# Value copies taken bank by bank during their unit, an output weight rounded ahead of the exponentials, and another order of output fills

## The reference, cut to what matters

```python
def dilated_attention_mixer(x, positions, k_sh, v_sh, w_q, w_o):
    q = rope((x @ w_q).reshape(...), positions)
    for g, (window, dilation) in enumerate(BRANCHES):   # (128,1), (512,4), (2048,16)
        o, lse = dilated_branch(q[:, :, g], k_sh[:, :, g], v_sh[:, :, g], window, dilation)
        ...
    wts = jax.nn.softmax(jnp.stack(lses, axis=0), axis=0)
    o = jnp.einsum("gbsh,gbshd->bshd", wts, jnp.stack(outs, axis=0))
    return o.reshape(B, S, N_HEADS * HEAD_DIM) @ w_o
```

## Time and profile before

| | us |
|---|---|
| median of 3 runs | 2104.25 (2101.3 to 2106.06) |
| the profiled execution's own time | 2102.27 |
| its span | 2100.5 |
| TensorE busy | 2063.2 (98% of the span) |
| VectorE busy | 1162.4 (55%) |
| ScalarE busy | 707.0 (34%) |

### The profile page before, as it was taken

The page is one execution under the profiler, slowest core; times in us unless marked ns, Lnnn a source line. Parts: engine busy times, 40 slices in busy tenths (PEclk is TensorE's granted clock), DMA queues, the critical chain, the costliest instruction groups (busy, mean ns, idle before and its releaser), DMA issues.

```text
span 2100.5 us, 26015 instructions
## 1 busy us (share of the span) xinstructions
PE 2063.2 (98%) x10218; PEld 1722.3 (82%) x10218; DVE 1162.4 (55%) x1954; ACT 707.0 (34%) x1088; POOL 9.7 (0%) x23
## 2 busy tenths in 40 slices
PE   8999999999999999999999999999999899999998
PEld 6888888888888898898887888888888678888886
DVE  6646444422774766757757744442398866444323
ACT  4224322221522323333234422231344563222213
POOL 0000000000000000000000000000000000000000
PEclk9999999999999999999999999999999999999999
DMA  5862222222124142151332122222222122222221
GB/s 175 117 112 81 100 100 100 100 100 96 67 104 135 61 129 72 61 140 61 108 94 68 59 95 100 100 100 100 100 102 81 41 100 81 100 86 95 101 98 60
DMA packets 37193, 198.53 MB, mean 95 GB/s; under 512 B 3911, under 2 KB 7016, under 8 KB 15736
## 3 DMA queue, kind: packets, MB, share of 16 engines
q1 hardware_dynamic: 28192, 179.91, 24.6%
q10 hardware_dynamic: 7992, 14.80, 3.1%
q0 software_dynamic: 928, 2.70, 2.6%
HBM read 181.14 MB, written 3.67 MB: 88 GB/s over the span
## 4 chain that ended last, share of the span: by engine, by line
PE 92%; DVE 4%; ACT 2%; issue 1%; DMA 0%; ACTq 0%; DVEq 0%
PE bank L1670 79%; PE bank L1711 5%; PE bank L1989 2%; PE bank L1951 1%; PE bank L1967 1%; PE bank L1700 1%; ACT w_hi L544 1%; DVE work L1005 0%; DVE w_lo L957 0%; DVE w_lo L959 0%; PE bank L2225 0%; PE bank L2130 0%; PE bank L2006 0%; DVE work L1070 0%; DVE h L1073 0%
## 5 line engine op out<-in xcount | busy, mean ns | idle before, releaser
L1670 PE MATMUL bank<-x_hi,w_hi 128*128 128x512 f32 x1564 | 619.9, 396 | 0.0
L1670 PE MATMUL bank<-x_hi,w_lo 128*128 128x512 f32 x1564 | 609.8, 390 | 0.0
L1670 PE MATMUL bank<-x_lo,w_hi 128*128 128x512 f32 x1564 | 609.3, 390 | 0.0
L957 DVE TENSOR_TENSOR w_lo<-w_raw,w_hi 128x2048 fp32r<-128x2048 f32 (+1 forms) x143 | 300.8, 2111 | 427.6 <-ACT w_hi L544 427.4
L544 ACT ACTIVATE w_hi<-w_raw 128x2048 fp32r<-128x2048 f32 (+1 forms) x132 | 249.9, 1895 | 341.2 <-PE bank L1670 318.5
L1670 PEld LDWEIGHTS bank<-x_hi,w_hi 128*128 128x128 f32 x1564 | 294.0, 188 | 65.2 <-issue 5.9
L1670 PEld LDWEIGHTS bank<-x_hi,w_lo 128*128 128x128 f32 x1564 | 293.8, 188 | 62.7
L1670 PEld LDWEIGHTS bank<-x_lo,w_hi 128*128 128x128 f32 x1564 | 294.3, 188 | 60.0 <-issue 1.4
L1670 PE MATMUL bank<-ff_hi,w_hi 128*128 (+2 forms) x542 | 208.1, 384 | 0.0
L1670 PE MATMUL bank<-ff_lo,w_hi 128*128 (+2 forms) x542 | 207.9, 384 | 0.0
L1670 PE MATMUL bank<-ff_hi,w_lo 128*128 (+2 forms) x542 | 207.9, 384 | 0.0
(11 more groups left out here) (225 smaller groups left out, 2295.4 us busy)
## 6 DMA issues: line engine op xcount, KB each, us to landing
w_raw<-w_all SPq DMA_DIRECT2D x167, 1024.0 KB, 4.9
qk<-qk_next ACTq DMA_DIRECT2D x32, 384.0 KB, 10.7
w_raw<-w_all SPq DMA_DIRECT2D x6, 256.0 KB, 8.7
h<-x_t ACTq DMA_DIRECT2D x3, 512.0 KB, 7.3
skew<-erow POOLq DMA_DIRECT2D x8, 192.0 KB, 8.8
out_t<-h SPq DMA_DIRECT2D x3, 512.0 KB, 3.0
bias<-skew POOLq DMA_DIRECT2D x8, 128.0 KB, 6.3
w_raw<-w_all SPq DMA_DIRECT2D x4, 128.0 KB, 3.7
```

What stands on the lines that cost most here:

```text
L957: ins = v.tensor_tensor(w_lo[p][:, part], raw, hi, ALU.subtract)
L1670: ins = mm(out, b if flip else a, a if flip else b, start=start and n == 0, stop=stop and n == 2, **kw)
```

## The change

`v12_unit` signals a new semaphore `v12_bank` when half 1 has finished banks 4, 5 and 6. VectorE takes those three quarters in a new `take_v12_banks`, which stands ahead of the group's start and waits bank by bank; each take counts in `v12_taken`. Only quarter 3 is taken inside the attention, at entry S1. TensorE's single wait before MAXPERM becomes three: for quarter 0 before MAXPERM, for quarters 0 and 1 before the first transpose, and for all four before the first product with the values. In the last group ScalarE rounds `ATT_OUT + 1` right behind `ATT_OUT`, ahead of the exponentials; VectorE makes its rest after entry S0, not S1; and the first four fills go half 0 of rows 0, half 0 of rows 1, half 1 of rows 0, half 1 of rows 1.

```diff
--- before.py
+++ after.py
@@ -220,6 +220,8 @@
 
 def fill_of(n):
 
+    if FILL_A <= n < FILL_A + 4:
+        return 0, (n - FILL_A) % 2, (n - FILL_A) // 2
     if FILL_A <= n < FILL_A + 2 * KC:
         return 0, (n - FILL_A) // 2, (n - FILL_A) % 2
     if FILL_B <= n < FILL_B + KC:
@@ -405,6 +407,8 @@
         at_av = sem("at_av")
         at_rl = sem("at_rl")
         at_out = sem("at_out")
+        v12_bank = sem("v12_bank")
+        v12_taken = sem("v12_taken")
         b_row = sem("b_row")
         b_rowcopied = sem("b_rowcopied")
         b_scores = sem("b_scores")
@@ -757,12 +761,11 @@
             for b in range(6):
                 mix_hi_block(b)
             round_unit(ATT_OUT)
+            round_unit(ATT_OUT + 1)
             for n, (pair, names) in enumerate(GROUP_STEPS):
                 for name in names:
                     attend(3, pair, name)
-                if n == 0:
-                    round_unit(ATT_OUT + 1)
-                elif n == 19:
+                if n == 19:
                     mix_hi_block(6)
                 if n == 27:
                     act.wait_ge(at_scores, 8 * KC)
@@ -1293,8 +1296,13 @@
             def take_v12(t):
                 for br in (1, 2):
                     ins = take_v(br, t, V12_BANKS[t][:, (br - 1) * 256:br * 256])
-                if t == 3:
-                    ins.then_inc(evac, 1)
+                ins.then_inc(evac if t == 3 else v12_taken, 1)
+
+            def take_v12_banks(group):
+
+                for t in range(3):
+                    dve.wait_ge(v12_bank, 3 * group + t + 1)
+                    take_v12(t)
 
             def attend(group, pair, name):
                 def cnt(per, n):
@@ -1315,8 +1323,8 @@
                                                mask_b[:, m0:m0 + 256 - lo], -1.0,
                                                -NEG if it < 4 else nm0r[:, n:n + 1], ALU.add, ALU.min,
                                                (nm0 if it < 4 else nm)[:, n:n + 1]).then_inc(at_negmax, 1)
-                    if pair == 0 and int(name[1]) < 4:
-                        take_v12(int(name[1]))
+                    if pair == 0 and name == "S1":
+                        take_v12(3)
                     if name == "S7":
                         dve.wait_ge(at_negmax, cnt(16, 16))
                         v.tensor_tensor(cdiff, nm, nm0r, ALU.subtract).then_inc(at_diff, 1)
@@ -1389,6 +1397,7 @@
                 u0 = QKV + GROUP * g
                 if g > 1:
                     rest_unit(u0)
+                take_v12_banks(g - 1)
                 dve.wait_ge(unit_done, u0)
 
                 def rotate_unit(x):
@@ -1423,6 +1432,7 @@
             for b in range(6):
                 mix_lo_block(b)
             rest_unit(ATT_OUT)
+            take_v12_banks(3)
             dve.wait_ge(unit_done, ATT_OUT)
 
             for n, (pair, names) in enumerate(GROUP_STEPS):
@@ -1438,7 +1448,7 @@
                         dve.wait_ge(w_rounded, FFN_B + 1)
                     if n <= 30:
                         rest_parts(FFN_B, quarters(FFN_B)[(0, 1, 3)[n - 28]:last], last == 4)
-                if n == 1:
+                if n == 0:
                     rest_unit(ATT_OUT + 1)
                 elif n == 18:
                     rest_unit(ATT_OUT + 2)
@@ -1922,6 +1932,8 @@
                         k = half * (KC // 2) + n
                         ins = products(V12_BANKS[t][:], weights(u, n * 512, 512),
                                        x_hi[:, k, cols], x_lo[:, k, cols], k == 0, k == KC - 1, flip=True)
+                    if half and t < 3:
+                        ins.then_inc(v12_bank, 1)
                 ins.then_inc(unit_done, 1)
 
             def attend(group, pair, name):
@@ -1963,6 +1975,8 @@
                         src = p_slot(it, a)
                         if k:
                             pe.wait_ge(at_ptcopy, cnt(16, 2 * (k - 1) + a + 1))
+                        elif pair == 0:
+                            pe.wait_ge(v12_taken, 3 * group + 2)
                         for c in range(1 if it == 0 else 0, 2):
                             ins = nc.tensor.transpose(bank[4 + a][:, c * P:(c + 1) * P],
                                                       src[:, c * P:(c + 1) * P], ident[:])
@@ -1974,6 +1988,8 @@
                     t = it % 4
                     if k == 0:
                         pe.wait_ge(at_out, cnt(2, 1))
+                        if pair == 0:
+                            pe.wait_ge(evac, EV_QKV + EV_GROUP * (group + 1))
                     for a in range(2):
                         pe.wait_ge(at_ptcopy, cnt(16, 2 * k + a + 1))
                         for c in range(1 if it == 0 else 0, 2):
@@ -1992,7 +2008,7 @@
                 elif name == "MAXPERM":
 
                     if pair == 0:
-                        pe.wait_ge(evac, EV_QKV + EV_GROUP * (group + 1))
+                        pe.wait_ge(v12_taken, 3 * group + 1)
                     pe.wait_ge(at_negmax, cnt(16, 8))
                     for r in range(4):
                         for j in range(4):
```

## The result

The changed kernel takes 2089.03 us in the median (2088.34 to 2090.06, 4 runs), the kernel before 2102.78 us (2099.46 to 2106.06, 4 runs with the earlier three). The ratio is 0.9933, 95% interval 0.9922 to 0.9945: faster by 0.7%, or 13.75 us between the medians. Forecast were 13.26 us and 2091.0 us (2087.5 to 2096.5). The profiled execution took 2088.77 us, with a span of 2087.0. One of the six runs of experiment 1 took 2994.74 us at a mean granted clock of 0.644, and its number there goes by the other five.

The account below looks back on a forecast made before the run. TensorE, busy 98% of the span, was taken to bound the kernel; 8.48 us (groups 0 to 2) plus 4.78 us (last group) gave 13.26 us, so 2104.25 - 13.26 = 2091.0 us, range 2087.5 to 2096.5.

Parts of the forecast that it names:

- The bound and the place of the waits: TensorE, 98% busy, waits before MAXPERM in groups 0 to 2 (1.83, 1.82, 1.83 us) and 3.53 us in the last.
- Takes during the unit cost nothing: Three quarter takes, 0.83 us each, fit VectorE's idle time during the value unit; added waits cost 0, at most 0.1 us each.
- MAXPERM in the groups 0 to 2: Before the first pairs' MAXPERM: 5.48 us of waiting and 1.56 and 1.44 us of half clock go, together 8.48 us.
- The last group: MAXPERM there starts 4.78 us earlier: 3.53 us of wait, 1.4 us of half clock, less a new 0.2 us wait.
- VectorE's idle time ahead of S0: In the last group VectorE is idle from 1066.51, the unit ends at 1070.04, and the third take ends near 1068.
- Rival A: Waits go, but MAXPERM's small products or another light stretch still run slowed: gain 8.8 us, time 2095.4; chance 0.07.
- the rule weighed: A skill's rule that only longer idle gaps lower TensorE's clock; by it two falls stay and the sum loses 3.0 us.
- B: The last group still stalls, 3.53 us returning at MAXPERM with half clock: only 8.48 us remain, 2095.8; chance 0.05.
- C: The wait moves to the first transpose, where 5.48 us return: about 2096.5 with the clock terms kept; chance 0.04.
- D: TensorE's work without pauses is itself slowed, at most 3.4 us a fall, four falls making it slower than before; chance 0.02.
- The sum: 8.48 us from groups 0 to 2 plus 4.78 us from the last group give 13.26 us.
- The low end of the range: 2087.5 us, from a clock fall in the third group (1.5 us) and runs up to 3 us below their median.

Follow-up runs that it names:

- experiment 1: The changed kernel with VectorE's quarter takes back at entries S0 to S3, TensorE's waits still split by bank: 2089.69 us, ratio to before 0.9935.
- experiment 2: The changed kernel with TensorE's one wait for all four quarters back before MAXPERM, takes still moved: 2089.16 us, ratio 0.9932.
- experiment 7: The changed kernel with one wait for all quarters before MAXPERM and quarter 3 taken at S3: 2092.55 us, ratio 0.9951.
- experiment 3: The changed kernel with the last group's three edits undone (rounding, rest and order of fills as before): 2093.6 us, ratio 0.9952.
- experiment 4: The kernel before with only the last group's three edits (rounding, rest, order of fills): 2101.77 us, ratio 0.9996.
- experiment 6: The changed kernel with the second output unit rounded behind S0's exponentials again: 2093.12 us in one run.
- experiment 8: The changed kernel with the last group's quarters 0 and 1 taken earlier, stage 0's last fill later and the third output unit rounded at S0: 2088.44 us, ratio 0.9925.
- experiment 5: The changed kernel with the first four fills in the old order: 2089.21 us in one run.

## Why the prediction was right

*The bound and the place of the waits.* Right. The four waits were where they were read, and they were on the path: their microseconds came back in the time.

*Takes during the unit cost nothing.* Right: no product of the value unit was later, six instructions lasted 2.44 us, as the 0.83 us a quarter say, and the added waits left no trace (experiment 2, which has none of TensorE's added ones, is as fast).

*MAXPERM in the groups 0 to 2.* 3.39, 3.26 and 1.83 us were forecast, 3.45, 3.29 and 1.94 us came. The small excess is largely a matter of how the wait was read: records of matmuls overlap, so the idle time in brackets is a little shorter than what the next start loses (S0 to MAXPERM took 12.43 us for 10.53, 1.90 us for 1.83 in brackets; 1.05 us in brackets cost 1.10 us in experiment 7). The copy of the maxima was ready ahead of S4's scores by a few tenths, as worked out. What the prediction put down to one edit was open to two: experiments 1 and 2 show that either the split wait or the moved takes remove the wait at MAXPERM, and that only the latter keep the first transpose free of one.

*The last group.* 4.78 us forecast, 4.30 us measured. The term that was mis-sized is VectorE's idle time ahead of S0: the forecast took 3.5 us of lead over the end of the value unit from the kernel before, but that lead hangs on the landing of the transfers into `qk`. They landed 10.8 us ahead of the last group's S0 before the change (1059.14 and 1069.97), as in experiment 2 (1050.68 and 1061.53), and 8.2 us ahead of it in the profile of the changed kernel (1053.31 and 1061.46). It cost 0.4 us at S2's scores and carried on to MAXPERM. The new wait of 0.2 us at MAXPERM was forecast, and is 0.24 us. In experiment 2, where the transfers were in time, the gain is 14.68 - 9.99 = 4.69 us: the chain of the forecast was right to 0.1 us, and what it lacked is that a landing can vary so.

*Rival A and the rule weighed.* In the profile of the changed kernel all the falls behind these waits are gone, including one that nothing was done about: the 1.55 us before the second pair's MAXPERM in the last group are there before and after, with half clock behind them before and not after. That gave 0.76 us that the forecast did not have (1.4 us of clock less a new wait of 0.67 us for the rest of the third output unit, which the slow stretch had covered). Before, with its clock, and after:

```profile
1117.31 0.66 PE L1999 MATMUL bank<-st,ident 128*32 128x2 f32 x32 [1.55 <-DVE st L1314]
...
1117.31:1120.71 3.40, 3.40 (x50) 3.06 (x51) 2.96 (x5) 2.22 (x7) 0.00 (x0) 0.57 0.00 0
```

```profile
1104.47 0.66 PE L2015 MATMUL bank<-st,ident 128*32 128x2 f32 x32 [1.55 <-DVE st L1322]
...
1106.89 0.50 PE L1680 MATMUL bank<-mix_hi,w_hi 128*128 128x512 f32 x1 [0.67 <-DVE w_lo L960]
```

This 0.76 us is not shown to be the change's: experiment 2, which is the same there, had the fall (0.57).

All ten profiles together, all waits from 0.98 us on, by the idle time and by whether the granted clock in the 3.4 us from its end read under 1.00:

| idle time of TensorE | under 1.00 | where |
|---|---|---|
| 3.8 us | 10 of 10 | third block, all profiles |
| 3.5 us | 2 of 2 | rest of the output unit: before, experiment 3 |
| 1.8 to 2.1 us | 6 of 8 | before (3), experiments 4 (4) and 6 |
| 1.49 to 1.55 us | 6 of 10 | second pair of the last group: MAXPERM, in experiment 8 S2's scores |
| 1.20 to 1.43 us | 0 of 21 | third block (2 in each profile), first scores of group 0 in experiment 8 |
| 0.98 to 1.05 us | 0 of 4 | experiments 5 and 7 |
| none or under 0.6 us | 0 of 28 | first pairs' MAXPERM wherever it did not wait longer |

Left out are the last group's MAXPERM of experiments 3 and 6, which ran into the slow stretch behind the wait ahead of them (0.88 and 0.81), and the waits of 6.0 to 6.7 us at the program's start, behind which the granted clock reads 1.00 though in the profile after the change four products of 128x512 last 2.04 us there and 1.07 us soon after. In three of the six falls of the fourth row (experiments 3, 4 and 6, 0.85 to 0.89) TensorE kept its full clock for the first 2 us, and half clock began only near the next wait, of 0.67 us; they may belong to the two waits together.

So these falls belong to the waits: they go with them, and come back with them. One fall does not, the one near 622 us of the last section. The Trainium skill (TensorE: Matmul & The Clock Gate, "HAM oscillation — how this bites in real kernels") speaks of longer gaps than these as what brings the clock down; the traces here disagree, with 0.52 to 0.64 behind six of eight waits of about 1.9 us. Part 1 of that page of the Trainium skill, that the place of a clock change varies from run to run, fits: the same wait of 1.55 us in front of the same products had the fall in one profile and not in another. Why was not tried.

*Rivals B, C, D.* B is experiment 3 or 6 and did not happen in the change; C happens only with the takes left in place, and then costs 0.6 us a group. For D there is one stretch of half clock with TensorE busy, near 622 us, in the profiles before and after alike, so it cancels between them; from 631 to 1643 us after the change, with no pause over 1.55 us, the granted clock was 1.00, and it fell next behind the wait of 3.84 us in the third block.

*The time.* The sum was 0.24 us short of the spans' difference: 0.20 us more came in the groups 0 to 2, 0.48 us less in the last group, 0.76 us that no term had, and 0.24 us less in the rest of the program. That it came so near is in part luck, since the 0.76 us made up for the rest; and the stretch of half clock near 622 us, worth 3.3 us, happened to be in both profiles. The terms of the change itself are off by 0.5 us at most. The forecast of 2091.0 us is 2 us above the median, 1.5 us of it because it was set against the median of three runs of before, 2104.25 us; with a fourth that median is 2102.78 us. The low end of the range does not quite follow from its two terms, which give 2091.0 - 1.5 - 3 = 2086.5 and not 2087.5 us; the median is inside either way.

## What to carry to other kernels

When an engine waits once for a set of things, ask which of them the next instruction needs, and ask separately whether the copies could be made while the producer still runs: here each of the two was enough to remove the wait at MAXPERM, and only the trace showed what the other was worth. Then follow the freed engine to its next need, since the last group's edits alone gave nothing that could be told: TensorE came 2.4 us earlier, then waited for the next thing and ran at half clock behind it. And count behind a TensorE wait like these, of 1.5 us and more, the slow products that may follow it; in the forecast they were a third of the gain (4.4 of 13.3 us).

## What was not expected of the hardware

Eight tiny products stand ahead of the first values' unit (1x1, 16 records, 2.9 to 3.5 us with TensorE busy throughout). From within or right behind them the clock was at half for 6.8 us in the profiles before and after the change and of experiment 2, for about 3.4 us in experiments 3, 5, 6 and 8, and not at all in 1, 4 and 7. TensorE had not waited before them, and what decides it stays open. Group 0 started at 660.9 to 661.1 us in the first three and at 657.4 to 657.9 us in the last three, of kernels whose instructions are the same up to there: 3.3 us, where the runs of the kernel before spread over 7.8 us (2099.15 to 2106.96).

The eight transfers into `qk` land at times that differ by 2.6 us between runs with the same start of the group, and in experiments 3, 5, 6 and 8 the first scores of group 0 waited 0.2 to 1.2 us for them. A stretch that looks free of waits in one profile can be that close to one.
